# Forget-gate attention computed by feature, with the reciprocals of the softmax sums spread by ScalarE

## The reference, cut to what matters

```python
log_f = jax.nn.log_sigmoid(fgate + fox_forget_b)
c = jnp.cumsum(log_f, axis=1).transpose(0, 2, 1)
fox_o = causal_block_attention(to_heads(fq, 8), to_heads(fk, 8), to_heads(fv, 8), c)
...
s = jnp.einsum('bhqd,bhkd->bhqk', q, k) * scale
s = s + c[:, :, q0:q1, None] - c[:, :, None, :q1]
p = softmax(where(mask, s, min))
out = jnp.einsum('bhqk,bhkd->bhqd', p, v)
...
return jnp.concatenate([fox_o, diff_o], axis=-1) @ w_out
```

## Time and profile before

| | us |
|---|---|
| median of three runs | 992.8 |
| the profiled execution, span | 990.5 |
| TensorE busy in it | 986.0 (100%) |
| VectorE busy | 711.5 (72%) |
| ScalarE busy | 486.3 (49%) |
| GpSimd busy | 213.1 (22%) |
| forget-gate stage on TensorE, first scores to first product with fox's output | 268.89 to 301.93 |

### The profile page before, as it was taken

One profiled execution on the slowest core, in us unless ns is written; L12 is line 12 of the kernel. 1 busy time (PEld: TensorE's weight loads), 2 busy tenths in 40 slices (PEclk: granted clock), 3 DMA queues, 4 the chain that ended last, 5 costly groups with the idle time before them and its releaser, 6 DMA issues.

```text
span 990.5 us, 14542 instructions
## 1 busy us (share of the span) xinstructions
PE 986.0 (100%) x5302; PEld 835.5 (84%) x5302; DVE 711.5 (72%) x849; ACT 486.3 (49%) x621; POOL 213.1 (22%) x215
## 2 busy tenths in 40 slices
PE   9999999999999999999999999999999999999998
PEld 6888888888888888888888888888888888888887
DVE  6766666775788767676777998678875767667674
ACT  6534343664666543434545444365555445334342
POOL 3313232014100232323112600060000012223230
PEclk9999999999999999999999999999999999999999
DMA  9665656745425656565745625544536456556561
GB/s 316 224 212 169 212 169 214 253 131 190 129 85 170 209 173 210 171 205 177 247 154 174 204 94 200 188 145 147 168 121 220 130 184 230 172 178 201 179 210 42
DMA packets 121017, 178.53 MB, mean 180 GB/s; under 512 B 5760, under 2 KB 82112, under 8 KB 120848
## 3 DMA queue, kind: packets, MB, share of 16 engines
q1 hardware_dynamic: 120048, 174.86, 53.8%
q0 software_dynamic: 576, 1.39, 0.5%
q10 hardware_dynamic: 352, 1.73, 0.5%
HBM read 176.88 MB, written 2.64 MB: 181 GB/s over the span
## 4 chain that ended last, share of the span: by engine, by line
PE 99%; DMA 0%; SPq 0%; ACT 0%; issue 0%; DVE 0%
PE acc L662 11%; PE acc L666 10%; PE acc L665 10%; PE tp L863 10%; PE gu L863 10%; PE gu L868 5%; PE tp L868 5%; PE tp L662 4%; PE tp L666 4%; PE tp L665 4%; PE gu L662 3%; PE gu L665 3%; PE gu L666 3%; PE acc L1143 2%; PE acc L1146 1%; PE acc L1172 1%
## 5 line engine op out<-in xcount | busy, mean ns | idle before, releaser
L2002 DVE TENSOR_TENSOR wlo<-raw,whi 128x2048 fp32r<-128x2048 f32 x140 | 325.7, 2331 | 153.9 <-ACT whi L1363 152.4
L1363 ACT ACTIVATE whi<-raw 128x2048 fp32r<-128x2048 f32 x150 | 285.7, 1908 | 70.3 <-PE acc L666 22.7
L863 PE MATMUL tp<-act_in,whi 128*128 128x512 f32 x432 | 102.9, 390 | 0.0
L863 PE MATMUL gu<-act_in,whi 128*128 128x512 f32 x432 | 102.6, 390 | 0.0
L1899 POOL TENSOR_TENSOR tmp<-tmp 128x256 f32<-128x256 f32 x54 | 39.7, 736 | 275.8 <-DVE tmp L2123 275.8
L1901 POOL TENSOR_TENSOR sil<-sil,tmp 128x256 f32<-128x256 f32 x54 | 88.8, 1644 | 33.5 <-ACT sil L1434 33.5
L863 PEld LDWEIGHTS gu<-act_in,whi 128*128 128x128 f32 x432 | 80.9, 188 | 16.6
L662 PE MATMUL acc<-whi,hT_hi 128*128 128x512 f32 x240 | 94.0, 392 | 0.0
L665 PE MATMUL acc<-wlo,hT_hi 128*128 128x512 f32 x240 | 93.7, 390 | 0.0
L666 PE MATMUL acc<-whi,hT_lo 128*128 128x512 f32 x240 | 93.4, 389 | 0.0
L863 PEld LDWEIGHTS tp<-act_in,whi 128*128 128x128 f32 x432 | 79.8, 188 | 15.7
(11 more groups left out here) (379 smaller groups left out, 1845.8 us busy)
## 6 DMA issues: line engine op xcount, KB each, us to landing
raw<-in_w_in SPq DMA_DIRECT2D x96, 512.0 KB, 4.7
raw<-in_down SPq DMA_DIRECT2D x66, 512.0 KB, 4.1
raw<-in_gate SPq DMA_DIRECT2D x64, 512.0 KB, 4.4
raw<-in_up SPq DMA_DIRECT2D x64, 512.0 KB, 4.9
raw<-in_w_out SPq DMA_DIRECT2D x16, 512.0 KB, 4.7
raw<-in_w_branch_hg SPq DMA_DIRECT2D x8, 512.0 KB, 4.3
raw<-in_w_branch_attn SPq DMA_DIRECT2D x8, 512.0 KB, 4.8
post<-in_post_gains SPq DMA_DIRECT2D x3, 512.0 KB, 6.2
```

Source lines behind the costliest of these rows:

```text
L863: pe.matmul(banks[:, a, :], w_hi[:, i, a * P:(a + 1) * P], both, start=i == 0, stop=False)
L1363: act.activation(split_weights(k)[0], raw[:, k % RING, :], ACT.Copy).then_inc(hi_ready, 1)
L2002: dve.tensor_tensor(w_lo, raw[:, k % RING, :], w_hi.bitcast(F32), ALU.subtract).then_inc(lo_ready, 1)
```

## The change

Both heads of a forget-gate pair are held together by feature, as the differential pairs are: head 0 on partitions 0 to 63, head 1 on 64 to 127. Their scores are made on halves of TensorE's rows (64 rows each), and the decay is a bf16 matmul of its own of six rows for each head: c is split by GpSimd into three bf16 parts, against rows of ones. The values take v as stationary (64 columns for each head) and the turned weights as moving, so the output stands by feature at once. Its scaling must then be by column: VectorE makes the four reciprocals of a pair (`fox_reciprocals`), ScalarE spreads each over 64 columns (`fox_rows`), TensorE turns these two tiles along with the weights, they are copied out with them (512 columns instead of 384), and VectorE's `output` multiplies by them. ScalarE rounds the result (`fox_hi`), VectorE makes the rest (`fox_lo`). The fills 2 and 3 go. The places of many steps in the four queues change; the diff, cut to what the steps below speak of:

```diff
-AUG = 64 + 2
+AUG = 6
...
-FOX_BEHIND = {4: (1, 2), 5: (1, 2), 6: (1, 1), 7: (0, 0)}
+FOX_BEHIND = {4: (2, 1), 5: (2, 1), 6: (2, 0), 7: (0, 0)}
...
         def scores(p):
-                if kind == 1:
+                if kind < 2:
...
+                    if kind == 0:
+                        decay = [slice(64 * h, 64 * h + AUG) for h in range(2)]
+                        for h in range(2):
+                            pe.matmul(late_half(p, h), aug_q[decay[h], i, P:S], aug_k[decay[h], i, :], start=False,
+                                      stop=False, skip_group_check=True)
+                        for h in range(2):
+                            pe.matmul(early_half(p, h), aug_q[decay[h], i, 0:P], aug_k[decay[h], i, 0:P], start=False,
+                                      stop=False, skip_group_check=True)
...
         def turn_weights(p):
+                if pair(p)[0] == 0:
+                    pe.wait_ge(exp_done, p + 1)
+                    for h in range(2):
+                        for n in range(3):
+                            to = (n + 1) % 3 * P
+                            pe.transpose(turned[:, h, to:to + P], e_sb[:, h, n * P:(n + 1) * P], idn)
+                    pe.wait_ge(rden_ready, p + 1)
+                    for t in range(TT):
+                        mm = pe.transpose(turned[:, t, 3 * P:4 * P], fox_rden(p)[:, (1 - t) * P:(2 - t) * P], idn)
...
         def values(p):
+                    for h in range(2):
+                        pe.matmul(o[at[h], 0, :], v[0][:, at[h]], fox_pT[:, h, 0:P], start=True, stop=True,
+                                  skip_group_check=True)
...
+            pe.wait_ge(lo_ready, N_WOUT + 2)
             half(N_WOUT + 1, 0, wout_banks(1), 1, 0, tiles=[2, 3], first_j=1)
-            pe.wait_ge(o_out, 8)
-            fills(T_WOUT, from_proj(MIX), 2, 3)
             half(N_WOUT + 1, 0, wout_banks(1), 1, 1, first_j=1)
...
+            pe.wait_ge(fox_lo_ready, 3)
+            half(N_WOUT + 2, 0, wout_banks(0), 0, 0, tiles=[0, 1, 2], first_j=1)
+            pe.wait_ge(fox_lo_ready, 4)
```

On ScalarE, with its place in the queue:

```diff
+            def fox_rows(p):
+                n = 6 * (p % 2)
+                act.wait_ge(fox_recips, p - 3)
+                act.activation(heads(fox_rden(p), 4), per(rden[:, n:n + 4], 64), ACT.Copy).then_inc(rden_ready, 1)
...
                 exps(4)
+                fox_rows(4)
                 next_hi(N_WIN, 0, 21)
                 fills(T_WOUT, 0)
                 block_out(N_WIN, 0, 23)
...
                         exps(p + 1)
+                        fox_rows(p + 1)
+                    else:
+                        hi(N_WOUT + 3)
                     if p == 4:
                         next_hi(N_WIN, 0, 23)
+                    fox_hi(p)
```

On VectorE, its queue:

```diff
                 fill_scaled(T_WOUT, 0)
                 fill_scaled(T_WOUT, 1)
+                fox_reciprocals(4)
                 half_lo(N_WOUT, 1)
                 block_out(N_WIN, 0, 23)
                 fill_rest(T_WOUT, 0)
                 weights_out(4)
...
-                half_lo(N_WOUT + 1, 1)
-                reciprocals(6)
+                fox_lo(4)
+                fox_reciprocals(6)
                 maxima(7)
                 weights_out(6)
+                fox_lo(5)
                 output(6)
+                fox_reciprocals(7)
+                weights_out(7)
+                half_lo(N_WOUT + 1, 1)
+                output(7)
+                fox_lo(6)
                 half_lo(N_WOUT + 2, 0)
-                weights_out(7)
+                fox_lo(7)
                 half_lo(N_WOUT + 2, 1)
-                output(7)
...
-            fills(T_WOUT, 2, 3)
             lo(N_WOUT + 3)
```

More of the change, by code:

```diff
@@ L666, in three, with half @@
                 return pe.matmul(out, lo, w_hi, start=False, stop=stop)
-            def half(k, r, banks, j, t, u=None, tiles=range(4), first_j=0, after_first=None):
-                if t == 0 and tiles[0] == 0:
+            def half(k, r, banks, j, t, u=None, tiles=range(4), first_j=0, after_first=None, first_half=None):
+                if first_half is not None:
+                    pe.wait_ge(first_half, 1)
+                elif t == 0 and tiles[0] == 0:
                     pe.wait_ge(lo_ready, k + 1 + 3 * r)
@@ L984, in scores @@
                 for h in range(2):
[L985 to L997, removed]
+                    q, k = q_sb[:, h, :], k_sb[:, h, :]
+                    pe.matmul(late_half(p, h), q[:, P:S], k, start=True, stop=True)
+                    mm = pe.matmul(early_half(p, h), q[:, 0:P], k[:, 0:P], start=True, stop=True)
                 mm.then_inc(scores_done, 1)
@@ L1101, in diff_and_fox @@
                         pe.wait_ge(o_out, 7)
[L1102 to L1105, removed]
+                        half(N_WOUT + 1, 0, wout_banks(1), 1, 0, tiles=[0, 1], first_j=1, first_half=wout_first)
+                    weights_read(p)
                     if p < 6:
@@ L1725, in _ @@
             diff_and_fox()
-            hi(N_WOUT + 3)
-            fills(T_WOUT, 2, 3)
             hi(N_FFN2)
@@ L2011, in half_lo @@
                     ins.then_inc(lo_ready, 1)
+                elif k == N_WOUT + 1:
+                    ins.then_inc(wout_first, 1)
             def fill_scaled(u, i):
@@ L2234, in maxima @@
                 n = 4 * (p % 2)
[L2235 to L2236 removed]
+                dve.tensor_reduce(mx[:, n:n + 2], lt, AX, ALU.max)
                 dve.tensor_reduce(mx[:, n + 2:n + 4], el, AX, ALU.max).then_inc(max_found, 1)
@@ L2250, in weights_out @@
                     return
-                dve.tensor_copy(pT_sb[:, 1, :], turned[:, 1, 0:3 * P]).then_inc(pT_d, 1)
-                if pair(p)[0] == 0 and p != 6:
-                    reciprocals(p)
+                to, n = (pT_sb, 3 * P) if pair(p)[0] else (fox_pT, 4 * P)
+                dve.tensor_copy(to[:, 1, 0:n], turned[:, 1, 0:n]).then_inc(pT_d, 1)
             def late_reciprocals(p):
@@ L2294, in mix_rows, with fox_reciprocals, fox_lo @@
                                          op0=ALU.mult, op1=ALU.add).then_inc(mixed, 1)
-            def reciprocals(p):
+            def fox_reciprocals(p):
                 n = 6 * (p % 2)
                 dve.wait_ge(exp_done, p + 1)
-                dve.reciprocal(rden[:, n:n + 4], den[:, :]).then_inc(rden_ready, 1)
+                dve.reciprocal(rden[:, n:n + 4], den[:, :]).then_inc(fox_recips, 1)
+            def fox_lo(p):
+                dve.wait_ge(fox_hi_ready, p - 3)
+                dve.tensor_tensor(heads(act_lo[:, p - 4, :], 2), fox_scaled(p), heads(act_hi[:, p - 4, :].bitcast(F32), 2),
+                                  ALU.subtract).then_inc(fox_lo_ready, 1)
             def output(p):
```

160 lines of the change are left out of this document (85 added, 75 removed).

## The result

The changed kernel takes 998.75 us (median of six, 997.51 to 1002.27) against 995.67 us of the kernel before beside it: ratio 1.0044, interval 1.0029 to 1.0058 (the two medians alone make 1.0031). A second comparison (the last experiment) gives 997.82 against 992.44 us, ratio 1.0055 (1.0042 to 1.0068). The second is the better measure: its 18 executions of the kernel before lie between 992.11 and 992.95, while the six of the first fall into two at 992.8 and four at 995.6 to 996.1, of which there is no trace. So the change costs 4.4 us by the first ratio and 5.4 by the second; the forecast was 1.1 us slower, with a range that ended at 996.8.

A forecast was written before the change was run, and what follows sets the result against it. TensorE was taken as the bound: 1.9 us less work minus 1.3 of new waits is 0.6 earlier, but late loads turn x 1.1 later; 992.8 + 1.1 = 993.9 us, range 991.8 to 996.8.

The forecast's parts named there:

- Landing of N_FFN2+1: Behind the forget-gate stage: load issued at 300.6, takes 4.85 us, lands at 305.5; the norm starts at 309.7.
- Carried to the end, 1:1: From the turning of x onward: its 1.1 us delay passes unchanged through the norm's steps to the kernel's end.
- TensorE's work: Forget-gate pairs and fills: scores 0.13 less, turning 0.22 more, values 0.36 less a pair, fills 0.8 less; sum -1.9 us.
- the second rival: Value products on column halves don't overlap: 0.55 us more a pair, 2.2 in all, giving 996.1 us; chance 0.13.
- New waits on TensorE: Forget-gate pairs: 0.8 us idle at pair 4, 0.2 at pair 5, 0.1 and 0.5 at pair 7; 1.6 against 0.3 before.
- What was costed at nothing: GpSimd's splitting and two memory trips, start memsets, and TensorE's own use of the moved rests: no wait expected.
- Loads not last: Rival: N_FFN2+1's load doesn't end last, TensorE's own balance decides: 0.6 us less, 992.2 us; chance 0.17.
- Longer spreading by ScalarE: Rival: spreading keeps each pair waiting by pair 4's 0.8 us; about 1.7 us more, 995.6 us; chance 0.10.

The follow-up runs named there:

- the last experiment: The changed kernel, unaltered, measured again against the kernel before: 997.82 us, ratio 1.0055.
- the first trace: Profiled execution of the changed kernel in its first comparison against the kernel before, the longest of six; median 998.75 us, ratio 1.0044.
- the first experiment: The changed kernel with one rest early: second half of N_WOUT+1's rest behind pair 6's reciprocals, not pair 7's copy of weights; 994.18 us, ratio 1.0021.
- both rests early: The changed kernel with the second half of N_WOUT+1's rest and both halves of N_WOUT+2's made earlier on VectorE; 991.74 us, ratio 0.9993.
- the reciprocals first: On top of both rests early: pair 4's reciprocals ahead of the two fill scalings, pair 7's ahead of pair 6's output; 990.84 us, ratio 0.9984.
- VectorE's spreading: The changed kernel with VectorE, not ScalarE, spreading the four reciprocals over 64 columns each; 997.39 us, ratio 1.0045.
- the same with 8 products: The changed kernel with N_WOUT+1's second half rest early and 8 extra unused products ahead of the first transposes of x; 994.05 us, ratio 1.0016.
- the norm ahead: The changed kernel, loads still late, with the norm's first steps ahead of N_FFN2+1's rounding and rest on ScalarE and VectorE; 993.51 us, ratio 1.0010.
- only the loads late: The kernel before, with only SyncE holding back N_FFN2's and N_FFN2+1's loads; 997.25 us, ratio 1.0046.
- third load held: The changed kernel with only N_FFN2+2's load held until N_FFN2+1's has landed; 995.79 us, ratio 1.0044.

## Why the prediction was wrong

The direction, the place and the mechanism were right; two steps were wrong, and together they are the difference.

- **Landing of N_FFN2+1: mis-sized.** I took 4.85 us, from the issue to the end of the flow of data in before. From issue to the start of the rounding it took 7.8 us in the first trace and 7.16 in the second (300.36 to 307.52). Over all traces in which ScalarE waited for it, it took 5.35 to 5.39 us in four and 6.8 to 8.0 in seven. The view of DMA issues of the kernel before, over 296 to 303.5 (count, KB each, us from issue to landing), had the short value:

```profile
raw<-in_gate SPq DMA_DIRECT2D x1, 512.0 KB, 3.9
raw<-in_up SPq DMA_DIRECT2D x1, 512.0 KB, 4.9
```

The second half is issued 0.4 us behind the first, so the piece landed 5.3 us after its issue. 0.5 us were lost by reading the end of the flow for the landing, and the other 1.8 by taking one observation as the price. That observation was of N_FFN2's load, issued at 289.36; the prediction calls it "this very load", but the step was about N_FFN2+1's. The issue itself was forecast at 300.6 and came at 300.06 and 300.04. Issue and landing together put the norm 1.7 us later than forecast (311.36 instead of 309.7), and x 1.75 later.
- **"Carried to the end, 1:1": wrong.** With the wait the granted clock fell to half, and that cost 2.41 us in the last trace, 2.7 in the first (17.60 us from x at 318.05 to the next block at 335.65, against 14.87 in before) and 1.55 in the executions of the first experiment. None of my rivals had this. The forecast's 1.1, plus 1.75 and 2.41, is 5.3, the measured delay.
- **TensorE's work: right.** Scores 1.45 us from 272.65 to 274.10 (forecast 1.40; decay 0.27, mask 0.22), values 0.81 from 284.41 with starts in pairs, and 0.17 more ahead of them than the four transposes at 274.10 take (0.53 from 283.88 against 0.36), so 0.98 (forecast 0.90). The two more transposes cost 0.14 where nothing waits behind them (284.63 to 284.77 with both rests early), less than 0.22. With the reciprocals first TensorE came to fox's part 1.87 us early (31.40 us for the stage against 33.27 from 268.66); less the 0.3 of waits that I put on before, and with 0.2 that are left at pair 7 (0.83 us from its first transposes to those of the reciprocals, 292.78 to 293.61, against 0.66 in the row at 281.02), that is 1.8 of work against 1.9. That both heads' products overlap on column halves (0.067 us an instruction) speaks against the second rival. The trace again doesn't agree with the rule of the Trainium skill ("TensorE: Matmul & The Clock Gate", Part 3, The mechanism) that weight loads run beside matmuls only where the row groups differ: both heads use all rows, and their twelve weight loads lie between 284.41 and 285.04, beside the products. The gap of 0.10 at the change of rows (272.42 to 272.75, less 0.23) is there, as the Trainium skill ("TensorEngine Tiling (Array Packing)", Key Properties), by which a change of the tiling mode drains TensorE, would have it.
- **New waits on TensorE: right in place, too large.** Pair 4: ScalarE idled 1.41 us for the reciprocals in the first trace and TensorE 0.35 to 0.39 us (forecast 0.8); pair 7: 0.3 (forecast 0.5; 0.97 us from 293.32 to 294.29 in the last trace, against the same 0.66). TensorE was 1.2 us early at fox's part instead of 0.6. It made the wait for x longer and was worth nothing; it became a gain only when the loads were early.
- **What was costed at nothing: right.** No wait on GpSimd's splitting appears: its last copy ends at 239.1 in the first trace, and its second trip through memory, issued up to 246.5, lands 1.9 us later, 25 us ahead of the first use at 273.61.
- **The rivals.** "Loads not last" is what both rests early make of the kernel: 991.74, 0.8 under before (forecast for it 0.6). "Longer spreading by ScalarE" (995.6) is not the cause: VectorE's spreading left the loss at 1.0045.

What stays open is why the landing falls into two groups. It was long also where it met no other load's data: in the kernel with the reciprocals first, N_FFN2+1's load was issued at 294.58 and its data had nearly all come by 299.5, and ScalarE could start at 301.42. In half microseconds (us, granted clock, DMA share, GB/s):

```profile
299.00:299.50 0.50, 1.00 0.23 59
299.50:300.00 0.50, 1.00 0.07 16
300.00:300.50 0.50, 1.00 0.07 23
300.50:301.00 0.50, 1.00 0.19 39
```

From 299.5 to 300.5 0.07 of the sixteen engines' time was used, about the time of one of them, as if one were behind. That is only argued; it was not tried. One more thing goes with the groups: where N_FFN2's load was issued 7 us or more ahead, N_FFN2+1's landed in 5.3 to 5.4 us in all three traces (the kernel before, one rest early, and the same with 8 products); where it was issued 2.3 to 4.7 us ahead, the landing took 6.8 us or more in eight traces of ten, the norm ahead (7.0) among them. No run moved that distance alone.

## What to carry to other kernels

When a step is moved in a queue, price first what its end releases: two rests that were moved, still in time for their own consumers, released their loads 7 and 3.4 us later, and with the second load a chain of landing, rounding, rest and norm that had 0.35 us to spare. Take a transfer's price as the range over many loads of the profile, from issue to the first instruction that could use it, and not from one. A wait on TensorE of a few microseconds is to be priced with what the clock does behind it: where it fell, that was 1.3 us (only the loads late: 16.20 us from 315.09 to 331.29, against 14.87) to 2.7 us here, where the wait itself was forecast at 1.8.

## What the runs showed of the hardware

- In or just behind an idle time of TensorE the granted clock fell to half: products stood 0.43 us apart from 312.6 to 316.0 behind a wait of 2.08 us (one rest early), from 314.7 to 318.7 behind 3.89, and from 318.8 to 323.7 behind 4.52. The length of the wait alone doesn't decide it: behind 2.12 us (third load held) and 1.66 (norm ahead) the clock stayed at 1.0, and the kernel with one rest early lost it in five executions of eleven.
- The same 1 MB load landed in 5.35 to 5.39 us or in 6.8 to 8.0 us. Where a long one met no other data (the row groups of half microseconds above), its last part flowed at 16 to 23 GB/s.
- The second half of N_FFN2's load took SyncE 0.8 to 1.4 us to issue in the traces in which it was issued behind pair 7's weights in the changed kernel (1.44 and 1.39 in the two of that kernel), and 0.51 wherever its rest was early. Why is open.
